# Rotation tables in the MLP, one weight tile per attention slot, cuts between norm pieces, and a later mean, in a two-block transformer kernel

## The reference

```python
for l in range(DEPTH):
    h = rms_norm_2(x, norm_mix_pre[l])
    proj = h @ w_in[l]
    (c_q, c_kv, k_rope, sc_b, sc_c, sc_x, cf_a, cf_g, gm_u, gm_v, gate_logits) = jnp.split(proj, pts, axis=-1)
    y_a = mla_branch(c_q, c_kv, k_rope, cos, sin, ...) @ w_o_mla[l]     # low-rank norm, q/k/v, rotation, attention
    y_b = short_conv_branch(sc_b, sc_c, sc_x, sc_conv_w[l]) @ w_o_sc[l] # sc_b * conv3(sc_c * sc_x)
    y_c = conformer_branch(cf_a, cf_g, ...) @ w_o_cf[l]                 # silu(layer_norm(conv31(cf_a * sigmoid(cf_g))))
    y_d = gmlp_branch(jax.nn.gelu(gm_u), jax.nn.gelu(gm_v), ...) @ w_o_gm[l]
    g = jax.nn.sigmoid(gate_logits.reshape(B, S, N_BRANCH, D) + gate_b[l])
    merged = g[:, :, 0] * y_a + g[:, :, 1] * y_b + g[:, :, 2] * y_c + g[:, :, 3] * y_d
    x = x + rms_norm_2(merged @ w_out[l], norm_mix_post[l])
    gu = rms_norm_2(x, norm_ffn_pre[l]) @ w_ffn_in[l]
    f_g, f_u = jnp.split(gu, 2, axis=-1)
    x = x + rms_norm_2((jax.nn.silu(f_g) * f_u) @ w_ffn_out[l], norm_ffn_post[l])
```

## Time and profile before

| | |
|---|---|
| median of 3 runs | 2309.62 us (2307.52 to 2311.80) |
| profiled execution | 2310.19 us, span 2308.1 us |
| mean granted clock of TensorE | 0.965 |
| busy: PE, DVE, ACT, POOL | 2141.5, 1552.1, 1151.8, 489.6 us |
| PE waits for DVE's cut (L396 for L1572) | 18.3 us in 16 waits |
| second block's first matmul | 1217.03 us (layer 0), 1767.80 us (layer 1) |

### The profile page before, as it was taken

One profiled execution on the slowest core, in us unless ns is written; L12 is line 12 of the kernel. 1 busy time (PEld: TensorE's weight loads), 2 busy tenths in 40 slices (PEclk: granted clock), 3 DMA queues, 4 the chain that ended last, 5 costly groups with the idle time before them and its releaser, 6 DMA issues.

```text
span 2308.1 us, 42283 instructions
## 1 busy us (share of the span) xinstructions
PE 2141.5 (93%) x17432; PEld 1970.9 (85%) x17432; DVE 1552.1 (67%) x2301; ACT 1151.8 (50%) x1917; POOL 489.6 (21%) x628
## 2 busy tenths in 40 slices
PE   6999979999999998899998989989998999998998
PEld 3985549999999995589997889989997888998997
DVE  3657766777777756667776769756555677965554
ACT  3534444555655642555556555554444655554443
POOL 0011330333233002213321043202110124311110
PEclk8999999999999998999999999999999999998999
DMA  8535444555465443335553435544553433553552
GB/s 325 164 128 220 165 183 146 178 195 177 155 201 185 153 165 128 147 119 188 187 190 104 157 104 191 173 138 164 185 190 103 146 128 129 165 185 127 191 191 84
DMA packets 103199, 378.21 MB, mean 164 GB/s; under 512 B 11584, under 2 KB 11744, under 8 KB 101984
## 3 DMA queue, kind: packets, MB, share of 16 engines
q1 hardware_dynamic: 101520, 367.31, 46.7%
q10 hardware_dynamic: 1488, 8.20, 0.9%
HBM read 374.42 MB, written 1.05 MB: 163 GB/s over the span
## 4 chain that ended last, share of the span: by engine, by line
PE 35%; issue 8%; DVE 6%; POOL 3%; ACT 3%; POOLq 0%; DVEq 0%; ACTq 0%
PE ps L396 10%; PE ps L397 10%; PE ps L398 10%; DVE WL L1572 2%; PE ps L453 2%; POOL R L2521 1%; POOL R L2479 1%; ACT WH L968 1%; DVE RST L1608 1%; DVE TMP L1582 1%; PE ps L410 1%; DVE R L1582 1%; PE ps L411 1%; PE ps L416 0%; POOL X L2284 0%
## 5 line engine op out<-in xcount | busy, mean ns | idle before, releaser
L396 PE MATMUL ps<-X,WH 128*128 128x256 f32 x4384 | 1243.4, 284 | 13.6 <-DVE WL L1572 12.5
L397 PE MATMUL ps<-X,WH 128*128 128x256 f32 x4384 | 1228.7, 280 | 0.0
L398 PE MATMUL ps<-X,WL 128*128 128x256 f32 x4384 | 1225.8, 280 | 0.0
L1572 DVE TENSOR_TENSOR WL<-RAW,WH 128x1024 fp32r<-128x1024 f32 (+2 forms) x608 | 802.7, 1340 | 461.3 <-ACT WH L968 460.6
L396 PEld LDWEIGHTS ps<-X,WH 128*128 128x128 f32 x4384 | 826.9, 189 | 28.3 <-DVE WL L1572 17.6
L397 PEld LDWEIGHTS ps<-X,WH 128*128 128x128 f32 x4384 | 827.4, 189 | 1.4
L398 PEld LDWEIGHTS ps<-X,WL 128*128 128x128 f32 x4384 | 827.1, 189 | 0.0
L968 ACT ACTIVATE WH<-RAW 128x1024 fp32r<-128x1024 f32 (+2 forms) x608 | 625.7, 1047 | 383.7 <-PE ps L398 362.5
L1106 ACT ACTIVATE PB<-ps,SM 128x512 f32<-128x512 f32 (+1 forms) x152 | 87.7, 584 | 156.4 <-DVE SM L1745 156.2
L2326 POOL TENSOR_SCALAR R<-CONS,SM 128x128 f32<-128x128 f32 x128 | 84.4, 670 | 360.5 <-DVE SM L1755 360.5
L2418 POOL TENSOR_TENSOR TMP<-TMP 128x256 f32<-128x256 f32 x66 | 49.0, 742 | 438.3 <-ACT TMP L1288 434.8
(11 more groups left out here) (184 smaller groups left out, 2157.5 us busy)
## 6 DMA issues: line engine op xcount, KB each, us to landing
RAW<-w_dram SPq DMA_DIRECT2D x674, 512.0 KB, 3.8
RAW<-w_dram SPq DMA_DIRECT2D x16, 480.0 KB, 3.1
BIG<-big_dram ACTq DMA_DIRECT2D x4, 1024.0 KB, 5.1
RAW<-w_dram SPq DMA_DIRECT2D x8, 320.0 KB, 2.7
RAW<-w_dram SPq DMA_DIRECT2D x6, 384.0 KB, 3.0
XT<-x_dram ACTq DMA_DIRECT2D x2, 1024.0 KB, 10.9
CONS<-con_dram ACTq DMA_DIRECT2D x1, 1105.0 KB, 5.0
out_dram<-XT SPq DMA_DIRECT2D x1, 1024.0 KB, 3.9
```

The costliest lines, as they stand in the source:

```text
L396: e.matmul(out, a.hi, b.hi, start=start and i == 0, stop=False, skip_group_check=open_bank)
L397: e.matmul(out, a.hi, b.lo, start=False, stop=False, skip_group_check=open_bank)
L398: last = e.matmul(out, a.lo, b.hi, start=False, stop=stop and i == n - 1, skip_group_check=open_bank)
L1572: e.tensor_tensor(weights(i).lo, raw(i), weights(i).hi.bitcast(F32), ALU.subtract).then_inc(*w_lo.mark(i))
```

## The change

Five edits, all of order; the arithmetic is the same.

1. The tables get a place of their own in `SM` (it grows from 1100 to 1604 columns). A generator `tables` on VectorE issues their 16 instructions one at a time, each behind a down tile of the first block's last MLP; the one on ScalarE passes 18 down tiles and applies Sin twice at the nineteenth. The product with the signs stays in the second block.
2. The four cuts reached by `used()` behind the low-rank norm are placed one behind each root and one behind each pair of halves.
3. `others` yields between the tile of `sc_c` and that of `sc_x`, so each step has one weight tile; the mixing of tile n joins the step of the gate tile n. There are 12 steps as before; ten run in slots, and two (gate tiles 2 and 3) behind them.
4. `fill` pumps five taps instead of four, and the single taps inside `others` go.
5. The third branch's hooks start with an empty one: mean and centering behind step 1, scale and silu behind step 2.

```diff
@@ scalar @@
+            def tables():
+                for _ in range(18):
+                    yield
+                for n, out in enumerate((sinM, cosM)):
+                    q.wait_ge(*small("angle", n))
+                    e.activation(out, out, ACT.Sin).then_inc(*gated.mark("rope", n))
+                yield
...
                     else:
                         i = used()
+                        next(aside, None)
...
-                    feed_forward(("ffn", l, 0), conv_gate(("ffn", l, 0)))
+                    feed_forward(("ffn", l, 0), conv_gate(("ffn", l, 0)), aside=tables())
@@ scalar, behind norm2 @@
-                if l == 0:
-                    for n, out in enumerate((sinM, cosM)):
-                        q.wait_ge(*small("angle", n))
-                        e.activation(out, out, ACT.Sin).then_inc(*gated.mark("rope", n))
@@ scalar; vector alike @@
+                bk = [PS.take(), PS.take()]
                 for n, (C, name) in enumerate(LOWS):
                     lows[n].rstd(256, k.rst2[n])
+                    used()
                     for half in range(2):
                         high(S[0][:, 2 * n + half], C[:, half], ("low", l, n, half), scaled("low", l, n, half))
                     k.rst2[n].free = [scaled("low", l, n, 1)]
-
-                bk = [PS.take(), PS.take()]
-                for c in range(4):
                     i = used()
@@ scalar @@
                 def others():
                     for pair in range(2):
                         for n in (2 * pair, 2 * pair + 1):
                             bank, i = tile()
-                            pump(1)
-                            tile()
                             b = tmp.take()
                             q.wait_ge(*lin(i))
                             wait(b.free)
                             e.activation(b.ap, bank.ap[:, 0:256], ACT.Copy).then_inc(*copied.mark("sc", l, n))
+                            b.free = [convd("sc", l, n)]
+                            yield
+                            tile()
                             q.wait_ge(*convd("sx", l, n))
                             e.activation(SCY[:, n], b.ap, ACT.Identity, scale=scw[:, 1, n:n + 1]).then_inc(*conv0.mark("sc", l, n))
-                            b.free = [convd("sc", l, n)]
                             yield
                         for n in (2 * pair, 2 * pair + 1):
                             tile()
                             high(S[0][:, n], SCY[:, n], ("sc", l, n), convd("sb", l, n), after_s)
+                            PS.take()
+                            tmp.take().free = [pooled("gm", l, n)]
+                            high(S[1][:, n], GU[:, n], ("gm", l, n), pooled("gm", l, n))
                             yield
-                    for g in range(4):
-                        PS.take()
-                        tmp.take().free = [pooled("gm", l, g)]
-                        high(S[1][:, g], GU[:, g], ("gm", l, g), pooled("gm", l, g))
-                        yield
@@ scalar, vector, gpsimd @@
                 def fill():
-                    pump(4)
+                    pump(5)
                     next(rest, None)
...
-                free_s, _ = branch(0, (center, scale))
+                free_s, _ = branch(0, (lambda i: None, center, scale))
@@ tensor @@
+                def mix(g):
+                    bank = PS.take()
+                    q.wait_ge(*merged("vn", l, 1))
+                    wait(bank.free)
+                    for c in range(2):
+                        last = e.matmul(bank.ap[:, 128 * c:128 * c + 128], VN[:, c, 128 * g:128 * g + 128], wsT[:, g, :], start=True, stop=True)
+                    last.then_inc(*mixed.mark(l, g))
+                    bank.free = [convd("bs", l, g)]
@@ gpsimd @@
                         for n in (2 * pair, 2 * pair + 1):
                             used()
                             low(S[0][:, n], SCY[:, n], ("sc", l, n))
+                            b = tmp.take()
+                            q.wait_ge(*gated("gu", l, n))
+                            q.wait_ge(*convd("bs", l, n))
+                            e.tensor_tensor(GU[:, n], GU[:, n], b.ap, ALU.mult).then_inc(*pooled.mark("gm", l, n))
+                            low(S[1][:, n], GU[:, n], ("gm", l, n))
                             yield
```

More of the change, by code:

```diff
@@ L869, in others @@
                             bb.free = [convd("sb", l, n)]
+                            mix(n)
                             yield
-                    for g in range(4):
[L872 to L878, removed]
-                        yield
                 rest = others()
@@ L929, in center @@
                     bank.free = [convd("cen", l, 3)]
-                branch(0, S[0], [(y_lo("ot", l, n),) for n in range(4)], (center, lambda: sq[0].rstd(k.rst2[0])))
+                branch(0, S[0], [(y_lo("ot", l, n),) for n in range(4)], (lambda: None, center, lambda: sq[0].rstd(k.rst2[0])))
                 branch(2, S[1], [(x_lo("cf", l, n),) for n in range(4)])
@@ L1135, in attend, with feed_forward @@
                 highs(units[n - 1]["tile"])
-            def feed_forward(tag, gate, early=None, late=None):
+            def tables():
[5 more added lines that the diff above has]
+                yield
+            def feed_forward(tag, gate, early=None, late=None, aside=iter(())):
                 bk, steps = [], iter(())
@@ L1799, in attend, with tables, then, feed_forward @@
                         invert(i)
-            def feed_forward(tag, gate, early=None, late=None):
+            def tables():
+                c = 0
+                def then(ins):
+                    nonlocal c
+                    ins.then_inc(*small.mark("table", c))
+                    q.wait_ge(*small("table", c))
+                    c += 1
+                q.wait_ge(s_pos, 16)
+                then(e.tensor_copy(KR, posb))
+                yield
+                q.wait_ge(s_con2, 16)
+                then(e.tensor_scalar(KR, KR, con("invf")[pr, 0:1], None, ALU.mult))
+                yield
+                for n, (out, turn_, shift) in enumerate(((sinM, 0.0, 0.0), (cosM, 0.25, math.pi / 2))):
+                    then(e.tensor_scalar(kf, KR, 1.0 / (2 * math.pi), turn_, ALU.mult, ALU.add))
+                    yield
+                    then(e.tensor_scalar(kf, kf, 12582912.0, None, ALU.add))
+                    yield
+                    then(e.tensor_scalar(kf, kf, -12582912.0, None, ALU.add))
+                    yield
+                    then(stt(out, kf, -6.28125, KR, ALU.mult, ALU.add))
+                    yield
+                    then(stt(out, kf, -0.0019353071795864769, out, ALU.mult, ALU.add))
+                    yield
+                    then(e.tensor_scalar(out, out, shift, 3.1415925, ALU.add, ALU.min))
+                    yield
+                    e.tensor_scalar(out, out, -3.1415925, None, ALU.max).then_inc(*small.mark("angle", n))
+                    yield
+            def feed_forward(tag, gate, early=None, late=None, aside=iter(())):
                 bk, steps = [], iter(())
@@ L1981, in vector @@
                         pass
-                    down = feed_forward(("ffn", l, 0), conv_gate(("ffn", l, 0)))
+                    down = feed_forward(("ffn", l, 0), conv_gate(("ffn", l, 0)), aside=tables())
                     add_ffn(0, down).rstd(k.rst[0])
@@ L2039, in vector @@
                         low(S[0][:, 2 * n + half], C[:, half], ("low", l, n, half))
-                PS.take(), PS.take()
-                for c in range(4):
                     used()
@@ L2119, in pump, with mix @@
                             tmp.take().free = [tapped3(l, j, 3)]
+                def mix(g):
+                    bank, b = PS.take(), tmp.take()
+                    q.wait_ge(*mixed(l, g))
+                    wait(b.free)
+                    for c in range(2):
+                        last = e.tensor_tensor(b.ap[:, 128 * c:128 * c + 128], bank.ap[:, 128 * c:128 * c + 128], bs[:, g, :], ALU.add)
+                    last.then_inc(*convd.mark("bs", l, g))
+                    b.free = [pooled("gm", l, g)]
                 def others():
@@ L2142, in others @@
                             e.tensor_tensor(SCY[:, n], bank.ap[:, 0:256], SCY[:, n], ALU.mult).then_inc(*convd.mark("sb", l, n))
+                            mix(n)
                             yield
-                    for g in range(4):
-                        bank, b = PS.take(), tmp.take()
-                        q.wait_ge(*mixed(l, g))
-                        wait(b.free)
-                        for c in range(2):
-                            last = e.tensor_tensor(b.ap[:, 128 * c:128 * c + 128], bank.ap[:, 128 * c:128 * c + 128], bs[:, g, :], ALU.add)
-                        last.then_inc(*convd.mark("bs", l, g))
-                        b.free = [pooled("gm", l, g)]
-                        yield
                 rest = others()
                 def fill():
-                    pump(4)
```

(1 more changed line is left out.)

48 lines of the change are left out of this document (12 added, 36 removed).

## The result

The changed kernel took **2329.52 us** (median of 4, 2326.28 to 2332.32) beside 2308.57 for the kernel before in the same sitting: a ratio of **1.0089** (95% interval 1.007 to 1.0108), slower by 21 us. The profiled execution took 2330.51 us, its span is 2328.3, 20.2 more than the span before; the mean granted clock is 0.963.

The account below looks back on a forecast made before the run. TensorE, busy 93% of 2308 us, was taken as the bound, so only its waits count. Terms -5.5 + 0.6 + 26.6 - 3.0 = +18.7 gave 2328.9 us in the profiled execution, 2328 as median, range 2318 to 2336.

Parts of the forecast that it names:

- the GpSimd chain behind the next reduction: Attention slots: gMLP product waits for diagonals, these for a reciprocal behind the next reduction; slots 5 and 6 wait 5.7 and 6.2 us.
- Tables, -5.5: Layer 0 of the second block: moving the rotation tables into the MLP gains 5.5 us, bounds -4.95 and -6.3.
- Splits, +0.3 a layer: Cuts between the low-rank pieces: the Gelu load starts later, +0.3 us a layer, +0.6 in all.
- Slots, +13.3 a layer: Attention slots: waits and cold clock of 25.3 us replace old waits of 12, +13.3 a layer, +26.6 in all.
- the walk: Slot-by-slot estimate of TensorE's waits in the new attention slots and behind the last one, summing to 22.1 us a layer.
- Mean a step later, -3.0 for both layers: Convolution mean: fewer taps and a later mean gain 3.0 us for both layers, bounds 0 and -5.
- six taps fewer remain, 2.0 us: Before the convolution mean: six taps fewer remain, five of them on VectorE at 0.4 us each, 2.0 us.
- Slots balance: Rival, attention slots: one tile a slot evens the load, no wait exceeds 0.7 us, total 2290; chance 0.11.
- A C wait is only 2.5: Rival: slots with a gate tile and mixing wait about 2.5 us, GpSimd's chain overlapping more; total 2310; chance 0.12.
- Each link waits out a tap: Rival: four GpSimd links in two mixing slots each wait 0.4 us, +5 a layer, 2338 and over; chance 0.07.

Follow-up runs that it names:

- step-first edit: The changed kernel with GpSimd's step of other work ahead of the two diagonals of its slot: 2313.95 us, ratio 1.0015 to the kernel before.
- both are mended: GpSimd's step ahead of its diagonals and the gMLP product's halves a step later, tables in the MLP: old slots 2295.51 us, new slots 2300.46.
- late high half: The changed kernel with high and low half of the gMLP product made at the head of the next step: 2303.08 us, ratio 0.9961.
- both edits: GpSimd's step ahead of its diagonals, gMLP product's halves a step later: on the changed kernel 2298.84 us; on old slots with tables in the MLP 2295.51.

## Why the prediction was right, and where it was off

The forecast was +18.7 us, 2328; measured was +21, 2329.5. The mechanism is the forecast's, the GpSimd chain behind the next reduction; that the total came within 2 us is in part luck, because two terms were off in opposite directions. Its terms one by one:

- **Tables, -5.5.** Alone -6.9 (-9.7 to -4.2); by the distance to the first Gelu -5.2 in that run (31.71 for 36.87). Right, with one detail wrong: Sin needed no table load in the MLP. It follows a Silu there, with only copies between, and ran at 1204.25 without one, so two loads went (Sin's own and the root's) and none came. The root of the changed kernel comes 16.94 us behind the first matmul, just under the 17 to 18 that were named. The rule of the Trainium skill (ScalarE: Activation LUTs, What ACT_TABLE_LOAD costs) would have made the term -6.9. The measured -6.9 happens to equal it, but its interval holds both, and the rows show no drain: the first Gelu began at 1253.82, 0.02 us behind the end of a load of 1.28 that began at 1252.52, itself 0.02 us behind the end of a cut.
- **Splits, +0.3 a layer.** Alone +0.5 in all. The stretch that it speaks of can be cut out: from the first low-rank root to the first Gelu all eight traces with splits take 14.1 us in both layers; of the twelve layers without, eight take 13.6 and four 14.0 to 14.2. So the splits cost up to 0.5 us a layer there, for the 0.3 forecast. TensorE's idle 2.00 us was no gain, as argued: it stands now in front of the products that wait for the Gelus.
- **Slots, +13.3 a layer.** Measured 14.6 and 16.2. The nine waits were forecast within 0.25 us each, but for the one behind the last slot, 3.71 for 2.9: the walk had left out that ScalarE's last cut itself stands behind GpSimd's product, and VectorE's product with `sc_b` behind that cut (its idle 3.13 at 1383.89). The halved clock fell in slots 5, 6, 8 and behind the last, not 2, 5, 6, and took some 2.8 us net inside the slots where 2.1 were counted.
- **Mean a step later, -3.0 for both layers.** Measured around the mean -3.9 and -2.6, -6.5 in all, outside the term's bounds of 0 and -5. The term was mis-sized: the step "six taps fewer remain, 2.0 us" is worth more. In the run of the slots alone, with the mean in place, they shorten its wait by 2.5 us (3.17 to 0.71), and the halved clock behind it goes too (the mean's eight matmuls take 1.96 us for 3.40), -4.1 and -2.6 us by stretches. The move of the mean, which the term is named for, adds nothing to that (28.54 for 28.33, 30.15 for 30.17) and costs 3 us alone. As forecast, no wait is left at the mean and one for a cut before it, of 1.97 us in layer 0 and 1.55 in layer 1 for the expected 2.5.

The errors had opposite signs: slots +4.2 over the forecast, mean 3.5 under it.

**The rivals.** "Slots balance" turned on ScalarE's high half of the product starting under 1.5 us behind the mixing; it started 4.3 behind the mixing's sum (1333.82 to 1338.10). "A C wait is only 2.5" is what the step-first edit makes of it (2.88 and 2.11): that rival had the product chain right and the diagonals in front of it wrong. "Each link waits out a tap", by the rule on the exclusive shared port in the Trainium skill (SBUF — State Buffer, Reading the diagram), would have given 7.3 and 7.8 in slots 5 and 6 (four links at 0.4 more). This rival failed on the meetings, not on the rule. In slot 5 tap, low half and product took 0.72 each and the pair of diagonals 1.19, and VectorE did nothing from 1334.73 to the values, so there was nothing to wait out. In slot 6 one link met VectorE, the diagonals, and cost 0.70. Where GpSimd's products and VectorE's cuts or taps do meet, the traces agree with the rule: the one that starts second ends a fixed time behind the end of the first, whatever its own start (the last section has the rows).

What stays open: whether the old slots beat the new ones once both are mended (5 us by medians, 0.1 by stretches of one trace each), what the late high half alone would do in the old slots, where only both edits were run together, and whether ten more taps in the old slots would win the mean's 4 to 5 us there as well. That wasn't run.

## What to carry to other kernels

A product handed from engine to engine inside a loop is priced by what each engine's queue holds in front of it, the work of the next iteration too. Here a 0.7 us multiplication cost 5 to 6 us of TensorE, because it stood behind diagonals that wait for the next reduction, and ScalarE's copy stood behind it. Before work is spread over the slots of such a loop, put the consumer of a foreign result a step later: that edit alone was worth 30 us here, more than the spreading, and together with the new order of GpSimd's step it took 7.6 us off the old slots as well. And a wait that is moved behind another instruction of the same queue is not removed: look at what released it, not at who waited.

## What the runs showed of the hardware

- VectorE's cuts and taps and GpSimd's 128x256 instructions with two tensors as input (taps, low halves, products) kept each other out for a whole instruction. With nothing beside them a cut takes some 1.23 us, a tap of VectorE some 0.47 and one of these GpSimd instructions some 0.73. In the traces before and after, 25 cuts start while one of the latter runs and no other follows beside them: all end 1.08 to 1.14 us behind its end. All 132 taps of VectorE that start so end 0.28 to 0.29 us behind its end. Ten of the GpSimd instructions start under a cut: all end 0.59 to 0.60 behind the cut's end. A cut that took 1.69 us and a GpSimd tap that took 1.57, in the kernel before, layer 0:

```profile
1337.44 0.73 POOL L2284 TENSOR_TENSOR X<-R,X 128x256 fp32r<-128x256 f32 x1
1337.58 1.69 DVE L1572 TENSOR_TENSOR WL<-RAW,WH 128x1024 fp32r<-128x1024 f32 x1 [1.35 <-ACT WH L968]
...
1355.56 1.22 DVE L1572 TENSOR_TENSOR WL<-RAW,WH 128x1024 fp32r<-128x1024 f32 x1 [1.16 <-ACT WH L968]
1355.80 1.57 POOL L2479 TENSOR_TENSOR R<-R,TMP 128x256 f32<-128x256 f32 x1
```

- TensorE's granted clock fell to 0.50 at the end of the wait of 5.57 us (1339.00) and inside the one of 6.30 (1349.20, 2.9 us before its end), but also behind one of 2.39 (slot 8 of the changed kernel), and in the kernel before behind 2.17. The length of one wait doesn't decide it: with both edits the slots hold waits of 2.63 and 2.65 us, and the clock is 1.00 over layer 0's and 0.97 over layer 1's:

```profile
1302.43:1365.49 63.06, 54.29 (x466) 49.74 (x465) 50.63 (x98) 35.69 (x80) 28.61 (x36) 1.00 0.31 100
1844.30:1908.80 64.50, 55.68 (x466) 50.98 (x465) 50.65 (x98) 35.70 (x80) 28.61 (x36) 0.97 0.30 98
```

- With unchanged code one execution can place such stretches otherwise: 1175.14 us with 78.5 at half clock against 1180.61 with 88.7, to the last MLP of the first block. A gain of 2 to 3 us can't be read from one trace unless the stretch that holds it is cut out.
- Sin behind Silu, with only copies between, needed no table load (1204.25 in the changed kernel). Before the change it followed the norm's square root and took a load at 1220.16, and the next root one at 1238.41.
